# Stage ends by token tile in a one-core, float32 network of two blocks

## What is computed

```python
for i in range(2):                       # first block, x is 256 x 1024
    x = x + (short_conv_mixer, swa_sink_attention)[i](rmsnorm(x, norm_mixer[i]), ...)
    x = x + swiglu_ffn(rmsnorm(x, norm_ffn[i]), w_gate_up, w_down)      # width 2816
for i in range(2):                       # second block, ALPHA = 4 ** 0.25
    mix = (attention_mixer, mamba2_bidir_mixer)[i](x, ...)
    x = layer_norm(ALPHA * x + mix, ln1_g[i], ln1_b[i])
    x = layer_norm(ALPHA * x + squared_relu_mlp(x, w1, w2), ln2_g[i], ln2_b[i])   # width 4096
```

## Time and profile before

| | |
|---|---|
| median of 3 runs | 1426.09 us |
| the profiled execution | 1428.35 us |
| its span, first to last instruction | 1426.5 us |
| TensorE matmul busy | 1349.1 us, 95% |
| VectorE busy | 956.8 us, 67% |
| ScalarE busy | 725.4 us, 51% |
| GpSimd busy | 163.9 us, 11% |
| granted TensorE clock, mean | 0.968 of 2.4 GHz |

### The profile page before, as it was taken

How to read it: one execution, slowest core, us unless ns; L and a number is a source line. 1 busy time by engine, 2 the same in 40 slices (tenths; PEclk the granted TensorE clock), 3 DMA queues, 4 the chain that set the end, 5 groups by cost and what they waited for, 6 DMA issues and landing times.

```text
span 1426.5 us, 20118 instructions
## 1 busy us (share of the span) xinstructions
PE 1349.1 (95%) x8246; PEld 1187.5 (83%) x8246; DVE 956.8 (67%) x1122; ACT 725.4 (51%) x987; POOL 163.9 (11%) x195
## 2 busy tenths in 40 slices
PE   8999999998999999998899999989899888999997
PEld 7898888888888888788788888888888778888885
DVE  6766665567756655665866665697889885766565
ACT  4445544455555444434634444466767663344441
POOL 0000000005340000000000000011344352000000
PEclk9999999999799999999899999999999999999998
DMA  8564656634077666435045556634333313455552
GB/s 281 194 189 134 191 182 197 201 129 148 4 174 207 182 196 199 161 123 173 1 148 177 177 182 202 206 119 149 118 121 116 118 61 119 134 199 199 177 178 88
DMA packets 220315, 223.07 MB, mean 156 GB/s; under 512 B 7232, under 2 KB 204224, under 8 KB 220096
## 3 DMA queue, kind: packets, MB, share of 16 engines
q1 hardware_dynamic: 217472, 213.94, 46.6%
q10 hardware_dynamic: 1728, 5.76, 1.3%
q0 software_dynamic: 1024, 2.10, 0.9%
HBM read 220.72 MB, written 1.05 MB: 155 GB/s over the span
## 4 chain that ended last, share of the span: by engine, by line
PE 79%; DVE 13%; issue 3%; ACT 2%; POOL 2%; DMA 1%; POOLq 0%; DVEq 0%; SPq 0%; ACTq 0%
PE ps L415 23%; PE ps L515 19%; PE ps L417 12%; PE ps L427 4%; PE ps L428 4%; PE ps L429 4%; PE ps L770 3%; DVE ssm_taps L1570 3%; DVE wlo L1202 2%; DVE weight L1593 1%; PE ps L404 1%; PE ps L406 1%; PE ps L405 1%; PE ps L606 1%; PE ps L595 1%
## 5 line engine op out<-in xcount | busy, mean ns | idle before, releaser
L1202 DVE TENSOR_TENSOR wlo<-raw,whi 128x2048 fp32r<-128x2048 f32 x202 | 468.5, 2322 | 166.6 <-ACT whi L845 166.6
L415 PE MATMUL ps<-act,whi 128*128 128x512 f32 x1408 | 503.3, 401 | 8.8 <-DVE act L1240 4.9
L845 ACT ACTIVATE whi<-raw 128x2048 fp32r<-128x2048 f32 x202 | 385.2, 1908 | 70.0 <-PE ps L515 37.1
L417 PE MATMUL ps<-act,wlo 128*128 128x256 f32 x1408 | 397.4, 282 | 0.0
L415 PEld LDWEIGHTS ps<-act,whi 128*128 128x128 f32 x1408 | 266.8, 189 | 74.9 <-issue 7.2
L417 PEld LDWEIGHTS ps<-act,wlo 128*128 128x128 f32 x1408 | 268.6, 191 | 1.8
L897 ACT ACTIVATE low_sb<-ps 128x512 f32<-128x512 f32 x88 | 52.6, 598 | 240.1 <-PE ps L417 240.1
L1697 POOL TENSOR_SCALAR small<-small 128x2 f32<-128x2 f32 (+2 forms) x17 | 6.5, 382 | 1081.1 <-DVE small L1228 713.7
L1319 DVE TENSOR_TENSOR sum_sb<-ps,low_sb 128x512 f32<-128x512 f32 x88 | 60.6, 688 | 101.2 <-ACT low_sb L897 101.2
L515 PE MATMUL ps<-whi,hidhi 128*128 128x512 f32 x400 | 124.3, 392 | 0.0
L515 PE MATMUL ps<-wlo,hidhi 128*128 128x512 f32 x400 | 123.9, 391 | 0.0
(11 more groups left out here) (222 smaller groups left out, 2164.6 us busy)
## 6 DMA issues: line engine op xcount, KB each, us to landing
raw<-in_mlp_w SPq DMA_DIRECT2D x128, 512.0 KB, 4.4
raw<-in_ffn_w_gate_up SPq DMA_DIRECT2D x88, 512.0 KB, 5.0
raw<-in_ssm_w_in SPq DMA_DIRECT2D x50, 512.0 KB, 4.8
raw<-in_ffn_w_down SPq DMA_DIRECT2D x44, 512.0 KB, 4.9
raw<-in_conv_w_in SPq DMA_DIRECT2D x24, 512.0 KB, 5.9
raw<-in_attn_w_in SPq DMA_DIRECT2D x18, 512.0 KB, 4.7
raw<-in_ssm_w_out SPq DMA_DIRECT2D x16, 512.0 KB, 4.4
raw<-in_attn_w_qkv SPq DMA_DIRECT2D x12, 512.0 KB, 4.3
```

The costliest lines, as they stand in the source:

```text
L415: e.matmul(ps[:, b + f, :].rearrange("p (a n) -> p a n", a=2), hi[:, k, cols], act[:, :, k, :], start=k == 0, stop=False, skip_group_check ...
L417: last = e.matmul(ps[:, b + f, 0:T], lo[:, k, cols], act[:, 0, k, :], start=False, stop=k == KT - 1, skip_group_check=True)
L845: e.activation(whi[s][:, :], raw[s][:, :], ACT.Copy).then_inc(*rounded.up(c))
L1202: e.tensor_tensor(wlo[s][:, :], raw[s][:, :], f32(whi[s][:, :]), ALU.subtract).then_inc(*split.up(c))
```

## The change

- The down chunk of step t-1 no longer follows step t's up chunk at the last two steps: up(last-1) and up(last) stand together, then down(last-2), then the last two down chunks together (`last_downs`): both for token tile 0, then both for tile 1. A third hidden buffer is used in FFN.
- An output projection does its chunks 2 and 3 first for tile 0, then for tile 1; their results lie in banks 2, 3 and 0, 1.
- Tile 0 is summed, normed, transposed (`turn_tile`, between tile 1's last products) and split into high and low while tile 1 is multiplied; the norm's gain and shift are applied in the token layout from rows loaded by DMA (`load_rows`), for all norms but the input's.
- The next stage's first two chunks are begun for tile 0, in an FFN or MLP with the high products alone (`wide_high`, 256 columns instead of 512), then tile 1 is transposed and both are finished (`first_wide_chunks`, `first_token_chunks`).
- keep-warm matmuls at stage ends and the zeroing of accumulators go (the first down chunk starts them).
- The state-space stage begins with the gate chunk that was k2 of G = 0, then dt, then k0, k1, k3 without a gate chunk between.
- The bias flips go behind chunks 3 and 5 of the second attention. The output is stored in four halves of tiles.

```diff
+        def down_behind(t, last):
+            return last - 2 if t == last else t - 1 if 0 < t < last - 1 else None
         def ffn_up(c0, t, q):
-            return c0 + q if t == 0 else c0 + 2 + 3 * (t - 1) + q
+            return c0 + q if t == 0 else c0 + 2 + 3 * (t - 1) + q - (t == D_FF // 256 - 1)
         def ffn_down(c0, t):
-            return c0 + 2 + 3 * t + 2 if t < D_FF // 256 - 1 else c0 + 32
+            return c0 + 30 + max(t - D_FF // 256 + 3, 0) if t >= D_FF // 256 - 3 else c0 + 2 + 3 * t + 2
         def mlp_up(c0, t):
-            return c0 if t == 0 else c0 + 1 + 2 * (t - 1)
+            return c0 if t == 0 else c0 + 1 + 2 * (t - 1) - (t == D_FF2 // 256 - 1)
         def mlp_down(c0, t):
-            return c0 + 2 * t + 2 if t < D_FF2 // 256 - 1 else c0 + 31
+            return c0 + 29 + t - D_FF2 // 256 + 3 if t >= D_FF2 // 256 - 3 else c0 + 2 * t + 2
+        SSM_DT = SSM + 1
         def ssm_step(G, k):
-            return SSM + 1 + 6 * G + k
+            return SSM + 1 + 6 * G + k if G else SSM + (2, 3, 0, 4, 5, 6)[k]
...
+        def out_place(n, m):
+            if n < 2:
+                return ps[:, n, m * T:(m + 1) * T]
+            return ps[:, (2, 3)[m], (n - 2) * T:(n - 1) * T]
+        def project_place(n, m):
+            bank = n if n < 2 else ((2, 3), (0, 1))[n - 2][m]
+            return ps[:, bank, m * T:(m + 1) * T]
...
+            def wide_high(s, b, ks=range(KT), m=0, opens=True, fs=(0, 1)):
+                hi, tile = w8(whi[s]), slice(m * P, (m + 1) * P)
+                for f in fs:
+                    out = ps[:, b + f, :].rearrange("p (a n) -> p a n", a=2)[:, :, tile]
+                    for k in ks:
+                        last = e.matmul(out, hi[:, k, f * P:(f + 1) * P], act[:, :, k, tile], start=k == 0 and opens, stop=False,
+                                        skip_group_check=True)
...
-            def turn_acts(n, src, ready):
-                if n != 4:
-                    keep_warm(24)
...
+            def turn_tile(n, m, js=(0, 1)):
+                src = h if n in (1, 2, 3) else x
+                for j in js:
+                    if n == 4:
+                        e.wait_ge(*added("ffn1", m, j))
+                    else:
+                        e.wait_ge(*scaled(n, m, j))
+                    for k in range(4):
+                        last = e.transpose(turn_bank(m, j)[:, k * P:(k + 1) * P], src[:, m, (4 * j + k) * P:(4 * j + k + 1) * P], ident)
+                    last.then_inc(*turned.up(n, m, j))
...
+            def first_wide_chunks(n, c):
+                for i in range(2):
+                    take(2 * i)
+                    take(2 * i + 1)
+                    e.wait_ge(*rounded(c + i))
+                    if i == 0:
+                        for j in range(2):
+                            e.wait_ge(*act_lo(n, 0, j))
+                            wide_high((c + i) % SLOTS, 2 * i, range(4 * j, 4 * j + 4), m=0)
+                    else:
+                        wide_high((c + i) % SLOTS, 2 * i, m=0, fs=(0,))
+                        if n < 4:
+                            turn_tile(n, 1, (0,))
+                        wide_high((c + i) % SLOTS, 2 * i, m=0, fs=(1,))
+                turn_tile(n, 1, (1,) if n < 4 else (0, 1))
+                for i in range(2):
+                    for j in range(2):
+                        if i == 0:
+                            e.wait_ge(*act_lo(n, 1, j))
+                        wide_high((c + i) % SLOTS, 2 * i, range(4 * j, 4 * j + 4), m=1, opens=False)
+                    e.wait_ge(*split(c + i))
+                    wide_low((c + i) % SLOTS, 2 * i).then_inc(*multiplied.up(c + i))
+                    free[2 * i] = free[2 * i + 1] = joined(c + i)
+            def first_token_chunks(n, c):
+                s, s2 = c % SLOTS, (c + 1) % SLOTS
+                take(s)
+                e.wait_ge(*split(c))
+                for j in range(2):
+                    e.wait_ge(*act_lo(n, 0, j))
+                    token_products(s, acthi, actlo, bank_of(s), 0, range(4 * j, 4 * j + 4))
+                    if n == 4:
+                        turn_tile(n, 1, (j,))
+                take(s2)
+                e.wait_ge(*rounded(c + 1))
+                for j in range(2):
+                    token_products(s2, acthi, actlo, bank_of(s2), 0, range(4 * j, 4 * j + 4), passes=(0, 2))
+                    if n != 4:
+                        turn_tile(n, 1, (j,))
+                for j in range(2):
+                    e.wait_ge(*act_lo(n, 1, j))
+                    last = token_products(s, acthi, actlo, bank_of(s), 1, range(4 * j, 4 * j + 4), opens=False)
+                last.then_inc(*multiplied.up(c))
+                e.wait_ge(*split(c + 1))
+                token_products(s2, acthi, actlo, bank_of(s2), 0, passes=(1,), opens=False)
+                token_products(s2, acthi, actlo, bank_of(s2), 1, opens=False).then_inc(*multiplied.up(c + 1))
...
+                for n in (2, 3):
+                    c = c0 + n
+                    place_of = lambda m, n=n: project_place(n, m)
+                    for q in range(4):
+                        last = token_products(c % SLOTS, mixhi, mixlo, place_of, 1, (2 * q, 2 * q + 1))
+                        if n == 3 and q < 2 and n_norm != 5 or n == 3 and q == 2 and n_norm == 5:
+                            turn_tile(n_norm, 0, (q % 2,))
+                    last.then_inc(*multiplied.up(c))
+                    if n == 3 and n_norm == 5:
+                        turn_tile(n_norm, 0, (1,))
+                for n in range(2):
+                    free[n] = added(st, 1, 3)
+                free[2], free[3] = added(st, 0, 2), added(st, 1, 2)
...
-            def open_accumulators():
-                for b in range(4):
-                    for half in range(2):
-                        e.matmul(ps[:, ACC + b, half * T:(half + 1) * T], zero[:, 0:P], zero[:, :],
-                                 start=half == 0, stop=False, skip_group_check=True)
...
+            def last_downs(st, before, hs_before, c, hs, hidden, n_norm):
+                for n in range(2):
+                    down_tile(before % SLOTS, hs_before, 0, n)
+                e.wait_ge(*split(c))
+                e.wait_ge(*hidden)
+                for n in range(2):
+                    down_tile(c % SLOTS, hs, 0, n).then_inc(*part.up(st, 0, n))
+                down_tile(before % SLOTS, hs_before, 1, 0)
+                if n_norm == 4:
+                    turn_tile(n_norm, 0, (0,))
+                down_tile(before % SLOTS, hs_before, 1, 1).then_inc(*multiplied.up(before))
+                if n_norm == 4:
+                    turn_tile(n_norm, 0, (1,))
+                down_tile(c % SLOTS, hs, 1, 0, (0,))
+                if n_norm == 2:
+                    turn_tile(n_norm, 0, (0,))
+                down_tile(c % SLOTS, hs, 1, 0, (1,)).then_inc(*part.up(st, 1, 0))
+                if n_norm == 2:
+                    turn_tile(n_norm, 0, (1,))
+                down_tile(c % SLOTS, hs, 1, 1, (0,))
+                if n_norm == 6:
+                    turn_tile(n_norm, 0, (0,))
+                down_tile(c % SLOTS, hs, 1, 1, (1,)).then_inc(*multiplied.up(c))
+                if n_norm == 6:
+                    turn_tile(n_norm, 0, (1,))
...
+                sz, s = SSM % SLOTS, SSM_DT % SLOTS
+                take(sz)
+                e.wait_ge(*split(SSM))
+                for j in range(2):
+                    e.wait_ge(*act_lo(6, 0, j))
+                    token_products(sz, acthi, actlo, bank_of(sz), 0, range(4 * j, 4 * j + 4))
+                e.wait_ge(*rounded(SSM_DT))
+                wide_high(s, s - 1, m=0, fs=(1,))
+                turn_tile(6, 1)
+                for j in range(2):
+                    e.wait_ge(*act_lo(6, 1, j))
+                    last = token_products(sz, acthi, actlo, bank_of(sz), 1, range(4 * j, 4 * j + 4), opens=False)
+                free[sz] = z_gated(0)
+                wide_high(s, s - 1, m=1, opens=False, fs=(1,))
+                e.wait_ge(*split(SSM_DT))
+                wide_low(s, s - 1, (1,)).then_inc(*multiplied.up(SSM_DT))
...
+                out_products(1, 2, 1).then_inc(*multiplied.up(ssm_out(1, 2)))
+                out_products(1, 3, 1, range(4))
+                turn_tile(7, 0, (0,))
+                out_products(1, 3, 1, range(4, 8)).then_inc(*multiplied.up(ssm_out(1, 3)))
+                turn_tile(7, 0, (1,))
                 for n in range(4):
-                    out_chunk(1, n)
-                    free[OUT_BANKS[n]] = added("ssm", 1, n)
+                    free[n] = added("ssm", 1, 3)
...
+            def next_stage(n, st, c, pieces):
+                for piece in pieces:
+                    square(st, 0, piece)
+                make_acts(n, 0)
+                hi(c)
+                for piece in pieces:
+                    square(st, 1, piece)
+                make_acts(n, 1)
...
+            def scale(n, m):
+                r = rms[n][:, m:m + 1]
```

(47 more changed lines are left out.)

691 lines of the change are left out of this document (318 added, 373 removed).

## The result

| | before | changed |
|---|---|---|
| median of the timed runs, us | 1427.51 | 1411.41 |
| their range | 1424.97 to 1430.47 | 1405.15 to 1415.91 |
| ratio, 95% interval | | 0.9889, 0.9848 to 0.9929 |
| a second round of six runs | 1427.58 | 1406.75 (1404.66 to 1416.74) |
| its ratio | | 0.9864, 0.9833 to 0.9895 |

The ten executions of the changed kernel have their median at 1407.0. They spread over 12 us; those of before over 5 in the first round and 11 in the second. By the medians of the two rounds the changed kernel is 16 to 21 us faster; in the profiled executions the difference is 21.1, where the prediction's sum said 19.

A forecast was written before the change was run, and what follows sets the result against it. TensorE, busy 95% of the span, bounds the kernel, with time to be had only at stage ends: 28 (inner ends) - 6.2 (state-space start) - 4.2 (clock) + 1.5 (tail) = 19 us, 1426.1 to 1407, range 1396 to 1418.

The forecast's parts named there:

- rival D: Split up products writing two PSUM runs cost up to 0.235 us instead of 0.12, making it slower: 1438 us; chance 0.04.
- E5: Stage end from second attention to MLP0: stalls of 2.8, 1.1 and 0.3 us left, 4.2 in all.
- E1: Stage end from conv to FFN0: stalls of 1.85 us left, 0.75 of it a bank wait on tile 1's last sum.
- E3: Stage end from sliding attention to FFN1: stalls of 1.85 us left, counted together with E1.
- E2: Stage end from FFN0 to sliding attention: stalls of 0.65, 0.15 and 0.8 us left, 1.6 in all.
- E4: Stage end from FFN1 to second attention: no norm there, so a stall of 0.
- E6: Stage end from MLP0 to state-space: stalls of 3.2, 0.95 and 0.5 us left, 4.7 in all.
- E7: Stage end from state-space to MLP1: same stalls as E5 with a later part signal, 5.0 us.
- the ceiling of 47.5: Most that can come off the stage ends: holes and warm-ups 37, zeroing 3.8, slow clock 6.5; 47 to 48 us.
- C: Holes return at the stage ends: VectorE's queue 1 us a tile longer, clock drops at every end; 1418 us, chance 0.19.
- B: Stalls fully covered: power not slowed, no clock given back, dt's steps overlap; 30 us off, 1396; chance 0.17.
- E: Stage ends stay as long because the next stage's first split comes last: within 3 us of 1426; chance 0.05.

The follow-up runs named there:

- the changed kernel's second profile: The changed kernel run again unaltered, beside three other kernels on one chip: 1406.75 us, ratio 0.9864 against the kernel before.

## Why the prediction was right, and where it was not

**What bounds the kernel.** Right. Steady chunks kept their period, all of the gain lies at the ends.

**Split products, rival D.** Dead. 32 of them take 4.07 us (E5 above), (4.07-0.28)/31 = 0.122 each, like a product into one run. The rule of "PSUM — Partial Sum Buffer", section "Specifications (TRN2)", in the Trainium skill, that any non-contiguous pattern slows matmuls significantly, does not hold for two runs of 128 fp32 columns 256 apart.

**Stalls left.** The order of events was right at every end, the sizes too high. E1 shows the bank wait on an addition (0.75 forecast) and the wait for tile 1's low part (0.5 forecast), and none ahead of the transposes:
```profile
111.14 3.11 PE L439 MATMUL ps<-act,whi 128*128 128x256 f32 x24 [0.69 <-DVE x L1362]
117.49 1.22 PE L439 MATMUL ps<-act,whi 128*128 128x256 f32 x8 [0.18 <-DVE act L1417]
```
That is 0.87 against 1.85, and E3 has 0.70 and 0.18. E2 has 0.45 against 1.6, E4 none, E5 2.57+0.97 against 2.8+1.1+0.3, E6 0.37+2.18+0.75 = 3.3 against 4.7, E7 the same 2.57 and 0.97 against 5.0: 12.6 us in all where 19 were charged. The prediction's own sign, first products of E1 to E4 within 2 us of idle in total, comes out at 2.2.

What failed at E1 and E3 is where the count began and what it left out. It followed each engine from project chunk 1 on. The new wait of conv's first project chunk on four banks comes one chunk earlier (1.94, with 1.5 of clock in this execution), and no weight load was costed as late, though 32 gathers run beside those of E3 (1.77). Without these two E1 and E3 bring 3.9 and 4.3, what the sum's mean of 4 for an end asks.

**The sum: in part luck.** In the prediction's own grouping, clock included (us):

| | forecast | profiled execution |
|---|---|---|
| seven inner ends (E6 2.7, E7 without the 1.9 ahead of it) | 28-1.5-1.2 = 25.3 | 22.0 |
| state-space start | -6.2-1.5 = -7.7 | -8.0 |
| tail | 1.5 | 2.9 |
| all other code | 0 | 1.1-1.7+1.5+1.5+1.9 = 4.3 |
| whole | 19 | 21.2 (21.1 without rounding) |

The ends brought 3.3 less than forecast, and 4.3 came from code in which the forecast had counted nothing, most of it clock that another execution of the same program may not give: from the second attention's second half the changed kernel's second profile gains 0.0 instead of 1.5. The ends should have brought more still: with the holes that are there (12.6, the 3.7 at conv and in FFN1, 3.0 of clock) the ceiling of 47.5 leaves some 27, not 22. Where the other 5 went stands in no hole of over 0.2 us, and stays open.

**E2 and what lies behind it.** E2 brought 4.1, but the sliding attention took 1.7 back. This step is missing from the prediction: behind the third chunk that stage waits for the head norms. Windows of its start, first before, then after:
```profile
330.00:350.00 20.00, 17.52 (x158) 16.84 (x156) 15.49 (x20) 12.03 (x17) 11.54 (x15) 0.99 0.51 159
```
```profile
330.00:350.00 20.00, 13.44 (x119) 12.45 (x117) 17.24 (x30) 12.66 (x31) 13.98 (x21) 0.89 0.45 142
```
TensorE came earlier and stood idle longer, 6.6 us of the 20 against 2.5; VectorE is the busier one. That the head norms do it was read from the chain alone, not tried. How much is taken back goes with the clock too: 0.7 to 0.9 us in four profiles with 17.1 us at the lower level in this stage, 1.5 to 1.7 in three with 27.3.

**GpSimd's power.** Mis-sized: the 0.6 for each layer norm is 0. All eight powers have a mean of 0.55 us, centring beside them.

**The state-space start.** Right in mechanism. The chain of 24.7 held in three kernels (24.5 each), the gate chunk alone costs 7.4 there in the kernel before (0.5 us ahead at chunk 134, 7.0 behind at 145), and the 6.2 charged is 3.6 (credited to E6) plus 2.6; measured, k0 ends 3.05 later relative to before, so E6 gave 2.7, and k4's copies come at the charged place. What makes the sum 5.3 instead of 2.6 is the half clock behind the hole (k4 takes 7.7 us instead of 5.9) and the 0.9 less from E6. The prediction had charged 1.5 for the clock at each of the two, apart from the 2.6; with them its sum for this place is 5.6, and this place was hit.

**Clock.** Forecast 4.2 back, in E5 to E7 and before k4. Found in the profiled execution: 1.5 at conv, 1.5 at E6, 1.8 at k4, and none at E5 and E7, whose 2.57 us did not drop it. The sum is near by chance of place. Over the eight profiles that have the same hole of 2.57 at E5 the clock fell behind it in five (1.3 to 1.5 us each) and at E7 in one: the 0.6 for each was a fair mean at E5, high at E7. Not forecast: stretches that before had in the second attention and in late state-space, up to the chunks ahead of E7, are gone, some 5 us of the 21 (13.7 us at half clock in the attention became 3.4, 6.8 at 1199.5 vanished). The other executions show that these come and go.

**Tail.** 2.9 against 1.5, over the bound of 2.5: 0.66 from the power that is no longer waited for, and the last tile's half-rows land 2.5 us behind their scaling, where before's rows took 3.2 (the prediction had read 2.7).

**The rivals.** C did not come true: VectorE's queue gave less stall than counted, not more, and the two holes that the count missed have other causes (a wait on four banks, late loads). B asked that dt hide in k1 and k3; it does not. E is excluded by the timeline of E5.
